# New start addresses modulo 128 B for the activation tiles of a two-block model on one core

## The reference

```python
proj = u @ in_w                      # 256 x 1024 by 1024 x several thousand
y = y.astype(u.dtype) @ out_w        # 256 x 2048 by 2048 x 1024
v = rmsnorm(h, g_ffn[i]) @ w_up[i]   # 256 x 1024 by 1024 x 5632
h = h + (jax.nn.gelu(v_gate) * v_val) @ w_down[i]
```

## Time and profile before

| | |
|---|---|
| median of three runs | 858.78 us |
| the profiled execution | 851.05 us |
| its span, first to last instruction | 849.3 us |
| granted TensorE clock, mean | 0.995 |
| TensorE busy | 830.9 us, 98% |
| weight loads busy | 798.9 us, 94% |
| POOL busy | 623.0 us, 73% |
| DVE busy | 528.2 us, 62% |
| ACT busy | 485.6 us, 57% |
| read from memory | 136.23 MB, 162 GB/s over the span |

### The profile page before, as it was taken

How to read it: one execution, slowest core, us unless ns; L and a number is a source line. 1 busy time by engine, 2 the same in 40 slices (tenths; PEclk the granted TensorE clock), 3 DMA queues, 4 the chain that set the end, 5 groups by cost and what they waited for, 6 DMA issues and landing times.

```text
span 849.3 us, 18278 instructions
## 1 busy us (share of the span) xinstructions
PE 830.9 (98%) x7055; PEld 798.9 (94%) x7055; DVE 528.2 (62%) x1543; ACT 485.6 (57%) x925; POOL 623.0 (73%) x282
## 2 busy tenths in 40 slices
PE   8999999999999999999999999999999999999995
PEld 8999988889999899999999998988999999999995
DVE  5997758883243635355358998876666666651164
ACT  6855476664546456564745466776655555554361
POOL 4899755665997465545798899635868888889781
PEclk9999999999999999999999999999999999999997
DMA  8677633331775444434475667433665666667611
GB/s 332 196 218 219 199 112 101 100 100 55 220 227 165 130 124 126 123 101 149 129 225 175 187 203 224 148 104 100 185 186 166 198 196 192 187 199 224 196 50 51
DMA packets 38679, 138.46 MB, mean 163 GB/s; under 512 B 4417, under 2 KB 4545, under 8 KB 38593
## 3 DMA queue, kind: packets, MB, share of 16 engines
q1 hardware_dynamic: 38592, 137.30, 52.6%
HBM read 136.23 MB, written 1.05 MB: 162 GB/s over the span
## 4 chain that ended last, share of the span: by engine, by line
PE 80%; DVE 2%; ACT 2%; issue 2%; POOL 1%; POOLq 0%; ACTq 0%; DVEq 0%
PE ps L640 21%; PE ps L642 21%; PE ps L641 21%; PE ps L862 1%; POOL wl L583 1%; PE ps L768 1%; PE ps L647 1%; PE ps L649 1%; PE ps L648 1%; PE ps L667 1%; PE ps L685 1%; PE ps L886 1%; ACT wh L1134 1%; PE ps L858 1%; PE ps L995 1%
## 5 line engine op out<-in xcount | busy, mean ns | idle before, releaser
L583 POOL TENSOR_TENSOR wl<-raw,wh 128x1024 fp32r<-128x1024 f32 x254 | 605.8, 2416 | 185.5 <-ACT wh L1134 185.3
L640 PE MATMUL ps<-uh,wh 128*128 128x256 f32 (+1 forms) x1248 | 351.1, 281 | 2.0 <-POOL wl L583 0.8
L642 PE MATMUL ps<-uh,wl 128*128 128x256 f32 (+1 forms) x1248 | 346.9, 278 | 0.0
L641 PE MATMUL ps<-ul,wh 128*128 128x256 f32 (+1 forms) x1248 | 346.8, 278 | 0.0
L1134 ACT ACTIVATE wh<-raw 128x1024 fp32r<-128x1024 f32 (+1 forms) x255 | 262.7, 1052 | 79.8 <-PE ps L642 69.9
L640 PEld LDWEIGHTS ps<-uh,wh 128*128 128x128 f32 (+1 forms) x1248 | 234.3, 188 | 4.3 <-issue 1.6
L641 PEld LDWEIGHTS ps<-ul,wh 128*128 128x128 f32 (+1 forms) x1248 | 234.7, 188 | 0.0
L642 PEld LDWEIGHTS ps<-uh,wl 128*128 128x128 f32 (+1 forms) x1248 | 233.9, 187 | 0.1
L1825 DVE TENSOR_TENSOR h<-ps,h 128x256 f32<-128x256 f32 x32 | 13.6, 425 | 97.8 <-PE ps L642 97.8
L1732 DVE SCALAR_TENSOR_TENSOR ps<-cpad,vec,ps 128x256 f32<-128x256 f32 x120 | 48.7, 483 | 0.0
L640 PE MATMUL ps<-ffh,wh 128*128 128x256 f32 x176 | 48.6, 276 | 0.0
(11 more groups left out here) (363 smaller groups left out, 1688.9 us busy)
## 6 DMA issues: line engine op xcount, KB each, us to landing
raw<-slabs SPq DMA_DIRECT2D x255, 512.0 KB, 4.2
h<-x_fm SPq DMA_DIRECT2D x4, 256.0 KB, 4.3
out_fm<-outb SPq DMA_DIRECT2D x4, 256.0 KB, 2.2
cst<-shape_consts SPq DMA_DIRECT2D x1, 768.0 KB, 8.1
vec<-vectors SPq DMA_DIRECT2D x1, 299.5 KB, 8.2
pin<-p_fm SPq DMA_DIRECT2D x1, 256.0 KB, 4.4
raw<-slabs SPq DMA_DIRECT2D x1, 128.0 KB, 2.3
vec<-vectors SPq DMA_DIRECT2D x1, 4.0 KB, 2.5
```

The costliest lines, as they stand in the source:

```text
L583: nc.gpsimd.tensor_tensor(wl[:, s % PART_RING, :], raw[:, s % RAW_RING, :], wh[:, s % PART_RING, :].bitcast(f32), ALU.subtract).then_inc(s ...
L640: nc.tensor.matmul(res, w_h, a_h, start=first, stop=False)
L641: nc.tensor.matmul(res, w_h, a_l, start=False, stop=False)
L642: ins = nc.tensor.matmul(res, w_l, a_h, start=False, stop=last)
```

## The change

ar gets an argument at, the place modulo 128 B at which a tile of 256 B or more starts. Tiles that are streamed by lines 640 to 642 get a value each; all others get 0. The alignment to 512 and 256 B goes. Where the place is not a multiple of 32 B, the allocation begins up to 28 B earlier and the tile is a view into it. Weights stay at 64. No instruction, wait, shape or order changes.

| tile | start modulo 128 | start minus weights, modulo 128 |
|---|---|---|
| uh, ul | 48 | 112 |
| ynh, ynl | 16 | 80 |
| ogh, ogl | 80 | 16 |
| cqh, cql, ckh, ckl | 8 | 72 |
| cnh, cnl | 96 | 32 |
| onh, onl, mh, ml | 32 | 96 |
| ffh, ffl | 112 | 48 |
| ph, pl | 64 | 0 |

```diff
-        def ar(name, shape, dt=f32):
+        def ar(name, shape, dt=f32, at=0):
+
             n = int(np.prod(shape)) * 4
             if n >= PIECE // 2:
-                cursor[0] += -cursor[0] % (PIECE if n >= PIECE else PIECE // 2)
-            t = nc.alloc_sbuf_tensor_at(name, [P] + list(shape), dt, offset=base + cursor[0])
-            cursor[0] += -(-n // 32) * 32
+                cursor[0] += (at - cursor[0]) % 128
+            lead = cursor[0] % 32
+            cursor[0] -= lead
+            if lead:
+                t = nc.alloc_sbuf_tensor_at(name, [P, (lead + n) // 4], dt, offset=base + cursor[0])
+                t = t[:, lead // 4:].rearrange("p (k t) -> p k t", k=shape[0])
+            else:
+                t = nc.alloc_sbuf_tensor_at(name, [P] + list(shape), dt, offset=base + cursor[0])
+            cursor[0] += -(-(lead + n) // 32) * 32
...
-        uh, ul = ar("uh", [KD, T], f32r), ar("ul", [KD, T], f32r)
+        uh, ul = ar("uh", [KD, T], f32r, 48), ar("ul", [KD, T], f32r, 48)
...
-        ynh, ynl = ar("ynh", [16, T], f32r), ar("ynl", [16, T], f32r)
+        ynh, ynl = ar("ynh", [16, T], f32r, 16), ar("ynl", [16, T], f32r, 16)
...
-        ogh, ogl = ar("ogh", [16, T], f32r), ar("ogl", [16, T], f32r)
+        ogh, ogl = ar("ogh", [16, T], f32r, 80), ar("ogl", [16, T], f32r, 80)
...
-        ffh, ffl = ar("ffh", [KF, T], f32r), ar("ffl", [KF, T], f32r)
+        ffh, ffl = ar("ffh", [KF, T], f32r, 112), ar("ffl", [KF, T], f32r, 112)
...
```

More of the change, by code:

```diff
@@ L362, in build @@
         kn, qn = ar("kn", [2, T]), ar("qn", [2, T])
-        cqh, cql = ar("cqh", [3, T], f32r), ar("cql", [3, T], f32r)
-        ckh, ckl = ar("ckh", [2, T], f32r), ar("ckl", [2, T], f32r)
+        cqh, cql = ar("cqh", [3, T], f32r, 8), ar("cql", [3, T], f32r, 8)
+        ckh, ckl = ar("ckh", [2, T], f32r, 8), ar("ckl", [2, T], f32r, 8)
         mx, nm, rs, rr = ar("mx", [2, 2]), ar("nm", [2, 2]), ar("rs", [2, 2]), ar("rr", [2, 2])
@@ L381, in build @@
         gm = ar("gm", [16, T])
-        cnh, cnl = ar("cnh", [4, T], f32r), ar("cnl", [4, T], f32r)
+        cnh, cnl = ar("cnh", [4, T], f32r, 96), ar("cnl", [4, T], f32r, 96)
         kcT, vcT = ar("kcT", [64]), ar("vcT", [P])
@@ L397, in build @@
         mt = ar("mt", [KD, T])
-        onh, onl = ar("onh", [4, T], f32r), ar("onl", [4, T], f32r)
+        onh, onl = ar("onh", [4, T], f32r, 32), ar("onl", [4, T], f32r, 32)
         npn, npT = ar("npn", [4, 3 * P]), ar("npT", [2, 3 * P])
-        mh, ml = ar("mh", [KD, T], f32r), ar("ml", [KD, T], f32r)
+        mh, ml = ar("mh", [KD, T], f32r, 32), ar("ml", [KD, T], f32r, 32)
         phase(after_u)
-        ffh, ffl = ar("ffh", [KF, T], f32r), ar("ffl", [KF, T], f32r)
+        ffh, ffl = ar("ffh", [KF, T], f32r, 112), ar("ffl", [KF, T], f32r, 112)
         fraw = ar("fraw", [4, T + FF_TAPS - 1])
@@ L407, in build @@
         pin = ar("pin", [2, T])
-        ph, pl = ar("ph", [2, T], f32r), ar("pl", [2, T], f32r)
+        ph, pl = ar("ph", [2, T], f32r, 64), ar("pl", [2, T], f32r, 64)
         psg, pt = ar("psg", [2, T]), ar("pt", [T])
```

## The result

The changed kernel takes 869.15 us (median of four runs, 869.05 to 870.51) against 855.73 of the kernel before (four runs, 852.5 to 859.03). The ratio is 1.0174 with a 95% interval of 1.0138 to 1.0211. The whole interval lies beyond the 1% within which the forecast saw no change: **slower**, by 1.4 to 2.1%. Whether it is more or less than 2% stays unclear. The time lies inside the stated range of 846 to 880, at the place of the collision rival (865 to 873).

What follows compares the result with a forecast made beforehand. TensorE's three projection products were taken to bound the kernel. Distance 0, own place +2 and writers 0 summed to +2 us: 857 us against 855, no change that can be told, range 846 to 880.

Steps and rivals of the forecast that it cites:

- collision rival: Products of lines 640 to 642: stream and weight load nearly meeting hold steps long; 865 to 873 us, chance 0.33.
- TensorE's pace is the time: Whole kernel: TensorE is busy 98% of the 849.3 us span and holds 80% of the chain.
- Distance priced at nothing: Projection products: the stream's distance to the weights likeliest costs nothing, bounds -8.0 to +17.8 us.
- the two levels: Projection products: a step takes 113.3 ns (short) or 117.8 ns (long), a state that disturbances switch.
- long steps: Projection products: some 1,790 of 5,784 steps take 117.8 ns, the other 3,990 take 113.3.
- the bounds: Distance cost of projection products: all steps short -8.0 us, all steps long +17.8 us.
- Modulo 128: Streamed tiles: distances to the weights taken modulo 128, all 64 before, then 112 for u and others per tile.
- Own place: Streams starting off a 128 B boundary may touch nine pieces instead of eight: 0 to +4.8 us, taken as 2.
- Writers: ScalarE, DVE and POOL writes to moved tiles: at most +0.5 us at the ends of norms, taken as nothing.
- freed rival: Projection products: new places let steps fall to the 111 ns floor, saving 21 us, 834 us; chance 0.15.
- States fall otherwise: Projection products: the new layout may re-deal short and long steps, inside 847 to 865 us; no separate chance.

Runs made afterwards that it cites:

- b: Changed kernel with 512 B alignment restored, weights at 96 and every streamed tile at 32 modulo 512 (distance 64 as before): 853.0 us, ratio 0.9975.
- c: Changed kernel with 512 B alignment restored, weights and all streams at 0 modulo 512 (distance 0): 879.17 us, ratio 1.0279.
- a: Changed kernel, tiles still aligned to 128 B, with every place back to 0: 861.39 us, 1.0072 times the kernel before.
- j: Changed kernel with 512 B alignment restored, weights at 64 and all streams at 256 modulo 512: 852.36 us, ratio 0.9971.
- l: Changed kernel with 512 B alignment restored, weights at 0 and all streams at 64 modulo 512: 867.42 us, ratio 1.0158.
- h: Changed kernel with 512 B alignment restored, weights at 64 and all streams at 128 modulo 512: 865.96 us, ratio 1.0116.
- e: Changed kernel with 512 B alignment restored, weights at 64 and all streams at 48 modulo 512: 865.54 us, ratio 1.0108.
- f: Changed kernel with 512 B alignment restored, weights at 64 and all streams at 32 modulo 512: 870.49 us, ratio 1.0165.
- p: As the distance-0 layout, but the low weights' product loads and computes half its outputs and stands second of three: 862.62 us, ratio 1.0053.
- o: Changed kernel with 512 B alignment restored, weights at 64 and all streams at 8 modulo 512: 880.37 us, ratio 1.0282.

## Why the prediction was wrong

*TensorE's pace is the time.* Right: busy shares and other engines stayed, TensorE still holds 80% of the chain, and the products' steps make up the whole difference.

*Distance priced at nothing: this step failed.* It rested on two rows, and neither was a test of it. The dt products have a quarter of the weights and took 116.7 ns, which I read as "the load does not matter". But dt's blocks of 32 columns lie 128 B apart, so their distance alternates between two values modulo 256, in every kernel here. In b, where all full products have 113.3, dt has ten steps in 1.20 us, 120.0:

```profile
8.41 0.28 PE L648 MATMUL ps<-ul,wh 128*32 128x256 f32 x1
...
9.61 0.28 PE L649 MATMUL ps<-uh,wl 128*32 128x256 f32 x1
```

In c, where all full products have 120.0, dt has six steps in 0.70 us, 116.7:

```profile
7.60 0.28 PE L648 MATMUL ps<-ul,wh 128*32 128x256 f32 x1
...
8.30 0.28 PE L648 MATMUL ps<-ul,wh 128*32 128x256 f32 x1
```

And in a, whose places of u and weights are those of before, 15 steps take 1.70 us, 113.3:

```profile
7.90 0.28 PE L648 MATMUL ps<-ul,wh 128*32 128x256 f32 x1
...
9.60 0.28 PE L648 MATMUL ps<-ul,wh 128*32 128x256 f32 x1
```

So at the same two distances dt took 113.3, 116.7 and 120.0. Its step varies by more than the two levels differ, for a reason that no run shows, and one reading of it can't price the load. The streams of 512 columns, from which I took that the excess goes with the stream and not the load, hardly react: in c nine steps take 2.06 us, 229 ns, against 230. Nor do they show the two levels that were read from them: the steps behind the earlier trace rows run from 225 to 232 ns one by one, and 230 is just their mean.

```profile
269.80 0.39 PE L656 MATMUL ps<-wh,ckl 128*128 128x512 f32 x1
...
271.86 0.39 PE L656 MATMUL ps<-wh,ckl 128*128 128x512 f32 x1
```

A step that takes twice as long over the same load is not the case that the kernel consists of. The trace of before held every full product of 256 columns at the one distance 192; it could not price another, and the honest price was the whole range between the bounds, -8.0 to +17.8 us. The measured change sits at the upper one: the span grew by 18.1. That it does so within 0.3 us is in part luck. All long would have been 17.6 us by the triples, and a third level, which no bound held, gave the rest. The long steps were counted a little high as well: a fifth of yn's and og's were taken as long, where 8 of 120 triples are.

*Modulo 128.* The prediction took over the 128 of the change. The runs fit 256, and high and low part have each a distance: u had 240 and 112, not 112 twice.

*Own place, +2 us.* Should have been nothing, its lower end, as far as it was tried: b (streams at 32) and j (at 256) have new places and no loss, and l (at 64) is as h (at 128).

*Writers, nothing.* Right. ScalarE's uh takes 494 ns as in the earlier trace rows, and TensorE's longest waits are the old ones:

```profile
L1162 ACT ACTIVATE uh<-h,vec x32: 491/494/508, 3.7 to 825.7; 128x256 fp32r<-128x256 f32 x32
...
PE ps L692 <- DVE root L1591: 2.5, 1, 2.5
PE ps L1108 <- ACT sq L1154: 1.9, 1, 1.9
```

*The collision rival* gave the sign and the time (865 to 873; all long is 851.05 + 17.8 = 868.9), but not the reason: there it was nearness, with u as the culprit. In fact u's 240 is among the milder distances (351.4 in e), and what mattered was leaving 192. That its price fitted is luck: it took the long step from before, and u came to the same 353 with other distances for its two parts. The tiles with a third level (yn and m at 120) were not foreseen.

*The freed rival* found nothing: of fourteen distances none is under 113.3. The isolated gap of N/2.4 + 2.5 ns that the Trainium skill gives ("TensorE: Matmul & The Clock Gate", section "Back-to-back issue gap"), by which 256 columns would take an estimated 109.2 ns, was not reached by the triples of any run.

*States fall otherwise.* They did, in a (861.39 us), and do in the kernel before itself, whose two groups of times lie some 8 us apart. That is less than the 13 us between the medians of before and after, and no execution of the changed kernel is below 869.05.

The Trainium skill, "SBUF — State Buffer", section "Who interferes with whom", gives TensorE two independent read ports, one for the stream and one for the weights, and has it never wait on anyone. Here moving the weights alone (before against c, b against f) changed the step of the same streams from 113.3 to 120.0 and 118.3 ns. The measurement decides: the two reads are not independent in their effect.

**Open.** What the two reads share; why 192 alone is good; what makes a stretch at 192 or 64 long or short. No run took the load away altogether, and p changes its length together with outputs and order, so a collision of addresses and a load that is slowed in itself are not told apart. Between the fourteen distances nothing was tried. The two groups of times of the kernel before may be its feed-forward stages in the short and in the long step, as in its trace (851.05 us) and in a's (861.97); only one of its executions was profiled, so that isn't shown. b and j tie with it by the intervals, though none of their 18 executions lies in the upper group (highest 855.14), where 19 of its 60 do.

## What to carry to other kernels

With full weight loads beside streams of 256 float32 columns, the start of the stream minus the start of the weights, modulo 256 B, moved the products of this kernel by up to 6% (113.3 to 120.0 ns): sweep it in the kernel itself, uniformly over all tiles and with the rest of the layout fixed, and keep high and low parts on the same place. Here that meant to align to 256 B or more, not 128. And when a trace holds a condition at one value only, rows from products of another shape don't price the other values: take the range between the bounds.

## What the hardware showed beyond that

At the distances 192 and 64 the pace has two levels, the same in all tiles (340.0 and 353.3 ns for three products), at distance 0 one (360.0). The two are sticky: with identical addresses ff took 113.3 a step in the kernel before and 117.6 in run a, for the whole stage, at a granted clock of 1.00. Work in between can turn either into the other: the same four products of a norm led u from short to long before, and from long to short in a. At other distances the three products of a triple can differ among themselves (yn after: 121.9, 118.5, 119.4; ff in o: 119.8, 125.0, 115.2), so a single step read from a timeline can mislead; the mean of triples doesn't.
